# A decoder step on one core: the order of the nine matmuls in each chunk of the MLPs

## What is computed

```python
def sq_relu_mlp(x, w_up, w_down):
    h = jax.nn.relu(x @ w_up)
    return (h * h) @ w_down

for l in range(DEPTH):                      # DEPTH = 2
    ...                                     # mLSTM mixer (l = 0) or window attention (l = 1), added to x
    x = x + sq_relu_mlp(rmsnorm(x, norm_ffn[l]), w_up[l], w_down[l])
```

## Time and profile before

| | |
|---|---|
| median of 3 runs | 2502.69 us (2500.77 to 2505.36) |
| the profiled execution's own time | 2495.87 us |
| its span, first to last instruction | 2496.7 us |
| TensorE busy with matmuls | 2415.8 us, 97%, 15530 matmuls |
| TensorE loading weights | 2310.6 us, 93%, 15530 loads |
| VectorE, ScalarE, GpSimd busy | 47%, 26%, 7% |
| mean granted TensorE clock | 0.988 of full |
| matmuls at L1606, the changed line | 9288 of the 15530 |

### The profile page before, as it was taken

The page is one execution under the profiler, slowest core; times in us unless marked ns, Lnnn a source line. Parts: engine busy times, 40 slices in busy tenths (PEclk is TensorE's granted clock), DMA queues, the critical chain, the costliest instruction groups (busy, mean ns, idle before and its releaser), DMA issues.

```text
span 2496.7 us, 36951 instructions
## 1 busy us (share of the span) xinstructions
PE 2415.8 (97%) x15530; PEld 2310.6 (93%) x15530; DVE 1172.6 (47%) x2055; ACT 655.3 (26%) x1096; POOL 162.5 (7%) x208
## 2 busy tenths in 40 slices
PE   6999999989999999999999999999999999999997
PEld 6899898878999999999999877878999999999997
DVE  6555555567433333333346675476434334334333
ACT  3233222334211111111213453353212112112113
POOL 3000000003000000000002010022000000000002
PEclk7999999999999999999999999999999999999999
DMA  3111121111111111111112311101111111111111
GB/s 107 49 44 57 47 65 38 44 36 43 43 43 51 44 43 51 44 43 51 43 43 62 94 34 41 34 18 40 46 51 43 43 51 43 43 51 43 43 51 70
DMA packets 177416, 120.55 MB, mean 48 GB/s; under 512 B 23623, under 2 KB 173044, under 8 KB 177220
## 3 DMA queue, kind: packets, MB, share of 16 engines
q1 hardware_dynamic: 177108, 118.10, 16.2%
q10 hardware_dynamic: 144, 0.02, 0.0%
HBM read 110.94 MB, written 12.33 MB: 49 GB/s over the span
## 4 chain that ended last, share of the span: by engine, by line
PE 73%; issue 19%; DVE 4%; POOL 2%; ACT 1%; DMA 1%; SPq 0%; POOLq 0%; ACTq 0%; DVEq 0%
PE acc L1606 59%; PE acc L1888 3%; PE acc L1890 3%; PE acc L1889 3%; PE acc L1907 2%; PE acc L1930 1%; PE acc L1918 1%; POOL small L991 1%; DVE rstd L1054 1%; DVE w_lo L1036 1%; DVE x_res L1193 0%; DMA out_y_prompt<-y_out 0%; DVE q_t L1441 0%; DVE prob L1475 0%; POOL small L989 0%
## 5 line engine op out<-in xcount | busy, mean ns | idle before, releaser
L1067 DVE TENSOR_TENSOR x_res<-x_res,acc 128x1056 f32<-128x1056 f32 x128 | 160.4, 1253 | 413.4 <-PE acc L1606 413.4
L1606 PE MATMUL acc<-x_hi,w_hi 128*128 128x352 f32 x1560 | 341.1, 327 | 13.4 <-DVE x_lo L1042 5.6
L688 ACT ACTIVATE w_hi<-w_raw 128x1024 fp32r<-128x1024 f32 x180 | 189.2, 1051 | 614.9 <-PE acc L1606 527.6
L1606 PE MATMUL acc<-x_hi,w_lo 128*128 128x352 f32 x1560 | 337.5, 324 | 0.0
L1606 PE MATMUL acc<-x_lo,w_hi 128*128 128x352 f32 x1560 | 337.4, 324 | 0.0
L1606 PE MATMUL acc<-h_hi,w_hi 128*128 128x352 f32 x1536 | 332.1, 324 | 0.0
L1606 PE MATMUL acc<-h_hi,w_lo 128*128 128x352 f32 x1536 | 331.1, 323 | 0.0
L1606 PE MATMUL acc<-h_lo,w_hi 128*128 128x352 f32 x1536 | 330.6, 323 | 0.0
L1606 PEld LDWEIGHTS acc<-x_hi,w_hi 128*128 128x128 f32 x1560 | 267.2, 190 | 16.8 <-issue 11.5
L1606 PEld LDWEIGHTS acc<-x_hi,w_lo 128*128 128x128 f32 x1560 | 268.9, 189 | 0.0
L1606 PEld LDWEIGHTS acc<-x_lo,w_hi 128*128 128x128 f32 x1560 | 266.4, 189 | 0.0
(11 more groups left out here) (265 smaller groups left out, 3085.8 us busy)
## 6 DMA issues: line engine op xcount, KB each, us to landing
w_raw<-in_w_up SPq DMA_DIRECT2D x64, 512.0 KB
w_raw<-in_w_down SPq DMA_DIRECT2D x64, 512.0 KB
w_raw<-in_w_mlstm_in SPq DMA_DIRECT2D x24, 512.0 KB
x_in<-in_x_prompt SPq DMA_DIRECT2D x8, 512.0 KB, 3.9
w_raw<-in_w_mlstm_out SPq DMA_DIRECT2D x8, 512.0 KB
w_raw<-in_w_q SPq DMA_DIRECT2D x16, 256.0 KB
w_raw<-in_w_attn_out SPq DMA_DIRECT2D x16, 256.0 KB
out_y_prompt<-y_out SPq DMA_DIRECT2D x8, 512.0 KB, 2.6
```

Source lines behind the costliest of these rows:

```text
L688: nc.scalar.activation(w_hi[:, s.parity], w_raw[:, s.parity], ACT.Copy).then_inc(hi_split, 1)
L1067: V.tensor_tensor(blocks(x_res[:, k]), blocks(x_res[:, k]), group(o), ALU.add).then_inc(out_taken, 1)
L1606: last = T.matmul(out[:, b], w[:, k, m], x[:, TN * b:TN * b + TN], start=(k == 0 and i == 0), stop=(k == k_chunks - 1 and i == 2))
```

## The change

In `chunk` the loop over the three banks becomes the outer one, and the loop over the three products the inner one. The nine matmuls, their operands, their flags and their targets stay the same, and so does the last of them, which signals the group of banks.

```diff
                 m = slice(P * n, P * n + P)
-                for i, (w, x) in enumerate(((hi, mh), (hi, ml), (lo, mh))):
-                    for b in range(TB):
+                for b in range(TB):
+                    for i, (w, x) in enumerate(((hi, mh), (hi, ml), (lo, mh))):
                         last = T.matmul(out[:, b], w[:, k, m], x[:, TN * b:TN * b + TN],
                                         start=(k == 0 and i == 0), stop=(k == k_chunks - 1 and i == 2))
```

## The result

The changed kernel takes 2479.46 us (median of 4 runs, 2474.78 to 2482.51), the kernel before 2502.34 (4 runs, 2500.77 to 2505.36). The ratio is 0.9906, with a 95% interval from 0.9886 to 0.9925. That is 22.9 us less; 26.2 were forecast, and 2476.5 us. Timed once more, as `e12_changed_again`, the ratio was 0.9894 (0.9878 to 0.9910), 2474.98 against 2500.35 us.

What follows compares the result with a forecast made beforehand. TensorE's matmul start rate was taken to bound the MLPs: 9,288 matmuls times 2.9 ns is 26.9 us, less 0.7 given back in waits, 26.2; so 2502.7 becomes 2476.5 us, with 8 in 10 from 2471 to 2491.

Steps and rivals of the forecast that it cites:

- What bounds the kernel, and that only the pitch can change: In the MLPs (L1606), TensorE's matmul start rate, 161.8 ns, sets the time; reordering can directly change only that pitch.
- The new pitch: MLP matmuls would start every 158.9 ns instead of 161.8, as in `dense` and `att_dense`; bounds 158.9 and 161.2 ns.
- the waits gave back: Where TensorE runs ahead of another engine, a shorter pitch lengthens its waits: 0.7 us in all, at three places.
- the 2.9 ns: Forecast saving per matmul on L1606, 161.8 - 158.9; over 9,288 matmuls 26.9 us.
- The rival of the slower rhythm: The MLPs run at 160.0 ns for much of their time: gain 16 us, 2487 us; chance 14%.
- the forecast case: The prediction's main case for the whole kernel: 2476.5 us, own range 2472 to 2481; chance 66%.
- a rhythm is kept until a wait breaks it: In unbroken MLP stretches of 1,000 to 2,000 matmuls, one bad phase at a start could hold for a third of an MLP.
- Loads of the stationary tile cost nothing extra, and were never saved: Weight loads equal matmuls, 15,530 each, and overlap in either order, so switching tiles six times per chunk costs nothing.
- The dearer switch: Rival: going from `w_lo` back to `w_hi` stalls the next matmul 17 ns; 35 us more, 2538 us; chance 5%.
- No change, because the pitch belongs to the place: Rival: 161.8 ns comes from the MLP's surroundings, not the sequence; 2502.7 us within some 5 us; chance 10%.

Runs made afterwards that it cites:

- e12_changed_again: The changed kernel itself, unaltered, timed again in the same rounds as the one with banks 0, 2, 1; 2474.98 us, ratio to before 0.9894.
- e1_weights_only: The kernel before with only the new sequence of weight tiles, at the old moving blocks and banks; 2498.53 us beside 2496.63 for before.
- e2_moving_only: The kernel before with only the new sequence of moving blocks, at the old weight tiles and banks; 2476.7 us, 19.9 under before.
- e5_old_order_aligned: The kernel before with odd blocks read 32 columns on or back, so every moving read starts at a multiple of 256 bytes; 2479.97 us beside 2497.79 for before.
- e6_new_order_shifted: The changed kernel with the second of three reads of each block shifted by 32 columns (128 bytes); 2496.15 us beside 2497.79 for before.
- e11_banks_0_2_1: The changed kernel with the banks of each chunk in the order 0, 2, 1; 2480.98 us over 6 runs, ratio to before 0.9917.

## Why the prediction was right

- *What bounds the kernel, and that only the pitch can change*: right. The MLPs gave 24.4 us, and no other engine's work changed.
- *The new pitch*: 158.9 ns forecast, 159.1 in the long stretch, because of the pieces in the slower rhythm. By that, 9,288 x 2.7 = 25.1 us, and the waits gave back 1.3 instead of 0.7; 23.8 is left, and the span is 23.7 shorter. The term of the sum that was too large is the 2.9 ns. Over several executions the saving was 22.9 and 25.4 us. The rival of the slower rhythm was thus partly true inside the forecast case: it is real, but held only some pieces of 46 us. What the prediction says of it, that a rhythm is kept until a wait breaks it, so that one bad phase could hold for 1,000 to 2,000 matmuls, is wrong: it changed after 288 matmuls, where the tiles go from `h` to `x` at 1850.08 us, without a wait.
- *Loads of the stationary tile cost nothing extra, and were never saved*: right by the counts, and `e1_weights_only` shows it by itself. The dearer switch is refuted. In the unbroken stretch of `dense` in the kernel before, L1688, the matmul after the switch, has a median of 322 ns:

```profile
L1688 PE MATMUL acc<-x_hi,w_hi x66: 322/322/395, 70.2 to 101.2; 128*128 128x352 f32 x66
```

  So the mean of 340 ns over all 576 comes from elsewhere, most likely from its restarts after waits.
- *No change, because the pitch belongs to the place*: refuted by the result. The Trainium skill ("TensorE: Matmul & The Clock Gate", "Back-to-back issue gap") gives N / 2.4 + 2.5 ns for an isolated matmul, an estimate of 149.2 ns for 352 columns, and says that in a stream of loads and matmuls both set the spacing. This kernel is such a stream, and no kernel with 352 columns came near the 149.2: measured are 158.9 and 161.8, and the difference between them lies in where the moving reads start.
- *What the forecast did not have*: a reason. It took the pitch from other code in the same kernel that had the same tiles, row length and sequence. To that extent it was luck: of the three sequences that the other code has in the new form only one counted. And it rests on the row length: with rows of another length the classes of the starts alternate differently. No other row length was run. The guess made after the result, that reading a block again at once helps, was wrong, though the run for it came out as it said (`e2_moving_only`); only `e5_old_order_aligned` and `e6_new_order_shifted` told the two apart.

Open: what chooses between the rhythms. The traces show where they change, at the joints between a piece on `x` and one on `h`, and not why. All of the MLPs' long stretches of before, and of the kernels with its moving sequence, ran at 161.8 ns; the others mostly ran at 158.3 to 160.0, and for some pieces at 161 to 167, with full clock and no wait. `e11_banks_0_2_1`, which I had thought could only be as good or better, had a slow piece in the first part of each of its two MLPs, and I did not find out why. Open too is which of the two readings of the classes holds. No kernel that was run beats the changed one by more than the measurement can tell.

## What to carry to other kernels

Where TensorE is the bound and matmul follows matmul, read the pitch, start to start, in the densest stretches of each part; two parts with the same tiles and different pitches show a gain before anything is built. Where blocks begin now at a multiple of 256 bytes and now 128 bytes off it, try a loop order in which that changes at most at every third matmul; here, with 352 float32 columns, that was 1.7% of the pitch, and making all starts alike gave nothing more. Other offsets, and the old order at another width, were not run. The order of the stationary tiles and of the PSUM banks could be chosen freely here. Separate the factors that a change moves together, by kernels that do not compute the right thing if need be, and then attack the reason too, since a run can come out as guessed for another one.

## What was not expected of the hardware

- The pitch of 352-column matmuls went with how often the start of the moving read alternates between 0 and 128 bytes modulo 256: from 1020 to 1320 us 158.9 to 159.4 ns with 0 to 6 changes in 18 matmuls, 161.6 to 161.8 with 14 to 18.
- An instruction stream can run in more than one steady rhythm: the same matmuls of `dense` at 158.9 ns and at 161.1 ns in two executions, and two parts of one MLP at 161.1 and 158.9 in one, with full clock and no waits. In the MLPs' pieces of 288 matmuls it changed where the stream goes from one kind of tile to the other; single pieces went from 158.3 to 166.6 ns in one kernel (`e5_old_order_aligned`).
- Beyond the columns at 2.4 GHz a matmul with its load of weights cost 12 to 15 ns more at 320, 352 and 384 columns (146.8 with some of 352 among them, 158.9, 174.8 ns).
